# A three-layer block on one Trainium2 core: the opening loads and turns by k tile

## The reference, cut to what matters

```
y  = rms_norm(x, ffn1_pre_g)                 # 256 x 1024
f1 = (silu(y @ w_gate) * (y @ w_up)) @ w_down    # w_gate, w_up: 1024 x 2816
x  = x + 0.5 * rms_norm(f1, ffn1_post_g)
```

## Time and profile before

| | us |
|---|---|
| median of 3 runs | 992.6 (992.57 to 992.99) |
| the profiled execution's own time | 992.94 |
| its span in the trace | 991.1 |
| TensorE busy in the span | 985.8 |
| first real product starts | 7.23 |
| `features` of piece 2 starts | 20.41 |

### The profile page before, as it was taken

How to read it: one execution, slowest core, us unless ns; L and a number is a source line. 1 busy time by engine, 2 the same in 40 slices (tenths; PEclk the granted TensorE clock), 3 DMA queues, 4 the chain that set the end, 5 groups by cost and what they waited for, 6 DMA issues and landing times.

```text
span 991.1 us, 14543 instructions
## 1 busy us (share of the span) xinstructions
PE 985.8 (99%) x5302; PEld 835.6 (84%) x5302; DVE 711.4 (72%) x849; ACT 486.5 (49%) x621; POOL 213.2 (22%) x215
## 2 busy tenths in 40 slices
PE   8999999999999999999999999999999999999998
PEld 6888888888888888888888888888888888888887
DVE  5766767775788767676777998677876767666664
ACT  6534343664665533434545444465555445334342
POOL 3313232014100222222112600060000012223230
PEclk9999999999999999999999999999999999999999
DMA  9665656745325555565745625544536356555561
GB/s 311 227 211 171 208 173 199 268 128 192 127 87 170 203 179 204 176 203 178 240 156 177 204 95 196 190 145 148 170 118 222 129 187 233 170 179 201 179 206 44
DMA packets 121065, 178.53 MB, mean 180 GB/s; under 512 B 5808, under 2 KB 82160, under 8 KB 120896
## 3 DMA queue, kind: packets, MB, share of 16 engines
q1 hardware_dynamic: 120048, 174.86, 52.8%
q0 software_dynamic: 576, 1.39, 0.5%
q10 hardware_dynamic: 400, 1.73, 0.5%
HBM read 176.88 MB, written 2.64 MB: 181 GB/s over the span
## 4 chain that ended last, share of the span: by engine, by line
PE 99%; DMA 0%; ACT 0%; SPq 0%; DVE 0%; issue 0%
PE acc L662 11%; PE acc L666 10%; PE acc L665 10%; PE tp L861 10%; PE gu L861 10%; PE gu L866 5%; PE tp L866 5%; PE tp L662 4%; PE tp L666 4%; PE tp L665 4%; PE gu L662 3%; PE gu L666 3%; PE gu L665 3%; PE acc L1141 2%; PE acc L1144 1%; PE acc L1170 1%
## 5 line engine op out<-in xcount | busy, mean ns | idle before, releaser
L2001 DVE TENSOR_TENSOR wlo<-raw,whi 128x2048 fp32r<-128x2048 f32 x140 | 325.5, 2330 | 153.8 <-ACT whi L1361 152.2
L1361 ACT ACTIVATE whi<-raw 128x2048 fp32r<-128x2048 f32 x150 | 285.8, 1908 | 70.2 <-PE acc L666 22.9
L861 PE MATMUL tp<-act_in,whi 128*128 128x512 f32 x432 | 102.9, 390 | 0.0
L861 PE MATMUL gu<-act_in,whi 128*128 128x512 f32 x432 | 102.6, 390 | 0.0
L1898 POOL TENSOR_TENSOR tmp<-tmp 128x256 f32<-128x256 f32 x54 | 39.8, 737 | 276.2 <-DVE tmp L2122 276.2
L1900 POOL TENSOR_TENSOR sil<-sil,tmp 128x256 f32<-128x256 f32 x54 | 88.7, 1642 | 33.7 <-ACT sil L1432 33.7
L861 PEld LDWEIGHTS gu<-act_in,whi 128*128 128x128 f32 x432 | 80.9, 188 | 16.6
L662 PE MATMUL acc<-whi,hT_hi 128*128 128x512 f32 x240 | 94.0, 392 | 0.0
L665 PE MATMUL acc<-wlo,hT_hi 128*128 128x512 f32 x240 | 93.7, 390 | 0.0
L666 PE MATMUL acc<-whi,hT_lo 128*128 128x512 f32 x240 | 93.4, 389 | 0.0
L861 PEld LDWEIGHTS tp<-act_in,whi 128*128 128x128 f32 x432 | 79.8, 188 | 15.7
(11 more groups left out here) (379 smaller groups left out, 1845.0 us busy)
## 6 DMA issues: line engine op xcount, KB each, us to landing
raw<-in_w_in SPq DMA_DIRECT2D x96, 512.0 KB, 4.5
raw<-in_down SPq DMA_DIRECT2D x66, 512.0 KB, 4.1
raw<-in_gate SPq DMA_DIRECT2D x64, 512.0 KB, 4.3
raw<-in_up SPq DMA_DIRECT2D x64, 512.0 KB, 4.7
raw<-in_w_out SPq DMA_DIRECT2D x16, 512.0 KB, 4.7
raw<-in_w_branch_hg SPq DMA_DIRECT2D x8, 512.0 KB, 4.3
raw<-in_w_branch_attn SPq DMA_DIRECT2D x8, 512.0 KB, 4.7
post<-in_post_gains SPq DMA_DIRECT2D x3, 512.0 KB, 6.0
```

The costliest lines, as they stand in the source:

```text
L861: pe.matmul(banks[:, a, :], w_hi[:, i, a * P:(a + 1) * P], both, start=i == 0, stop=False)
L1361: act.activation(split_weights(k)[0], raw[:, k % RING, :], ACT.Copy).then_inc(hi_ready, 1)
L2001: dve.tensor_tensor(w_lo, raw[:, k % RING, :], w_hi.bitcast(F32), ALU.subtract).then_inc(lo_ready, 1)
```

## The change

SP's list is new. It opens with `fixed`, then gate and up of k tile 0 (128 KB each), gate and up of k tile 1, the second quarter of x's columns for both row halves, then k tiles 2 and 3, then as before. ACT's queue opens with the first quarter of x's columns for t = 0 and t = 1 (128 KB each) and one merged array of one-hot and bias table. SP's list up to the first wait grows from 15 DMAs to 20, for the same bytes. TensorE turns two tiles of t = 0 and two of t = 1 at first, multiplies k tile 0 for both row halves, turns the other four tiles, and goes on by k tile. The bias product moves from ahead of the products to behind the fourth. Piece 1 is rounded in quarters instead of halves. `x_sums` for t = 0 moves behind the last `fills`. The first tiles' PSUM banks are others, and every tile has a semaphore step of its own.

The diff, cut to its core:

```diff
             def first_pieces():
-                x_part(0, 0)
-                half_piece(0, 0)
-                x_part(1, 0)
-                half_piece(0, 1)
+                sp.dma_start(fixed[:, 0:G_END + P], fixed_d[:, 0:G_END + P]).then_inc(head_in, 16)
+                for a in range(2):
+                    first_gate(a)
+                    first_up(a)
+                x_quarter(0, 1)
+                x_quarter(1, 1)
+                for a in (2, 3):
+                    first_gate(a)
+                    first_up(a)
                 x_part(0, 1)
...
                 pe.wait_ge(head_in, 16)
-                turn(0)
-                warm_up(3)
-                pe.wait_ge(bias_parts_in, 16 * 2)
-                pe.matmul(gu[0:8, 1, 0:S], rel[:, :], hot[:, :], start=True, stop=True).then_inc(row_product, 1)
...
+                for i in range(2):
+                    pe.wait_ge(x_first[i], 16)
+                    turn_tile(i, 0)
+                    turn_tile(i, 1)
+                    warm_up(2 - i)
+                pe.wait_ge(tile_lo, 1)
+                pe.wait_ge(part_hi, 1)
+                product(0, 0, 0, rests=(part_lo, 1))
+                pe.wait_ge(tile_lo, 2)
+                product(0, 1, 0)
+                pe.wait_ge(x_in[0], 16)
+                turn_tile(0, 2)
+                pe.wait_ge(x_in[2], 16)
+                pe.wait_ge(tile_lo, 3)
+                turn_tile(1, 2)
+                turn_tile(0, 3)
+                turn_tile(1, 3)
+                pe.wait_ge(part_hi, 2)
+                product(0, 0, 1, rests=(part_lo, 2))
+                pe.wait_ge(tile_lo, 4)
+                product(0, 1, 1)
+                pe.wait_ge(bias_parts_in, 16)
+                pe.matmul(acc[0:8, 1, 0, 0:S], rel, hot, start=True, stop=True).then_inc(row_product, 1)
...
-            first_turned(0, 0, 1, 2)
+            first_turned(0, 0)
             first_hi(0, 0, 1)
-            first_turned(0, 3)
+            first_turned(1, 0)
+            first_turned(0, 1)
             first_hi(0, 1, 1)
+            first_turned(1, 1)
+            first_hi(0, 2, 1)
+            for a in (2, 3):
+                first_turned(0, a)
+                first_turned(1, a)
+            first_hi(0, 3, 1)
             row_from_bank()
-            first_turned(1, 0, 1, 2, 3)
-            first_hi(0, 2, 1)
-            first_hi(0, 3, 1)
-            first_hi(1, 0, 2)
+            first_hi(1, 0, 1)
+            first_hi(1, 1, 1)
             fills(T_FFN1, 2)
+            first_hi(1, 2, 1)
+            first_hi(1, 3, 1)
+            fills(T_FFN1, 3)
             x_sums(0, 0)
-            first_hi(1, 2, 2)
-            fills(T_FFN1, 3)
             hi(2)
...
             fill_scaled(T_FFN1, 2)
-            first_lo(1, 0, 2)
+            first_lo(1, 0, 1)
             fill_rest(T_FFN1, 2)
             fill_scaled(T_FFN1, 3)
-            first_lo(1, 2, 2)
+            for a in range(1, 4):
+                first_lo(1, a, 1)
             fill_rest(T_FFN1, 3)
```

More of the change, by code:

```diff
@@ L172, in build @@
         same = rest[:, C_SAME - P:C_SAME - P + HALF]
-        hot = sb("hot", [REL_BUCKETS, S])
+        bias_parts = sb("bias_parts", [REL_BUCKETS, S + 8])
+        hot, rel = bias_parts[:, 0:S], bias_parts[:, S:S + 8]
         mask16 = sb("mask16", [P, P], BF16)
@@ L228, in build @@
         x_in = [sem(f"x_in{i}") for i in range(2 * TT)]
-        part_in = [sem(f"part_in{i}") for i in range(4)]
+        x_first = [sem(f"x_first{t}") for t in range(TT)]
+        part_in = [sem(f"part_in{i}") for i in range(6)]
         tile_turned, tile_hi, tile_lo = sem("tile_turned"), sem("tile_hi"), sem("tile_lo")
@@ L408, in first_bank @@
         def first_bank(i, a):
-            return tp[:, a // 2, a % 2 * P:(a % 2 + 1) * P] if i else acc[:, a // 2, a % 2, 0:P]
+            banks = (tp[:, 0, :], acc[:, 1, 0, :], acc[:, 0, 1, :], tp[:, 1, :]) if i else \
+                (acc[:, 0, 0, :], acc[:, 0, 1, :], acc[:, 1, 1, :], acc[:, 0, 0, :])
+            return banks[a][:, 0:P]
         def first_place(i, a):
@@ L746, in turn, with turn_tile @@
                     pe.wait_ge(x_in[2 * t + h], 16)
-                    if i >= 2:
-                        fill(u, i, from_x)
-                        return
-                    for a in range(4):
-                        mm = pe.transpose(first_bank(i, a), from_x(t, 4 * h + a), idn)
-                        if a < 3 and (i == 0 or a == 1):
-                            mm.then_inc(tile_turned, 1)
-                    mm.then_inc(turn_full, 1)
+                    fill(u, i, from_x)
+                def turn_tile(i, a):
+                    mm = pe.transpose(first_bank(i, a), from_x(FILLS[u][i][0], a), idn)
+                    mm.then_inc(turn_full if a == 3 else tile_turned, 1)
                 def product(j, t, a, rests=None):
@@ L767, in first_block @@
                 pe.wait_ge(head_in, 16)
[L768 to L783 removed]
+                for i in range(2):
[21 more added lines that the diff above has]
+                pe.matmul(acc[0:8, 1, 0, 0:S], rel, hot, start=True, stop=True).then_inc(row_product, 1)
+                pe.wait_ge(tile_lo, 5)
                 pe.wait_ge(part_hi, 3)
                 product(0, 0, 2, rests=(part_lo, 3))
+                turn(2)
+                pe.wait_ge(tile_lo, 6)
+                product(0, 1, 2)
+                filled(u, 1)
                 pe.wait_ge(hi_ready, 1)
@@ L788, in first_block @@
                 filled(u, 2)
-                product(0, 1, 2)
+                pe.wait_ge(row_copied, 1)
                 turn(3)
@@ L792, in first_block @@
                 filled(u, 3)
-                pe.wait_ge(part_hi, 4)
-                product(1, 0, 0, rests=(part_lo, 4))
-                product(1, 0, 1)
+                for a in range(3):
+                    pe.wait_ge(part_hi, 4 + a)
+                    product(1, 0, a, rests=(part_lo, 4 + a))
                 pe.wait_ge(hi_ready, 2)
-                product(1, 0, 2, rests=(lo_ready, 2))
-                product(1, 0, 3).then_inc(gu_first, 1)
+                product(1, 0, 3, rests=(lo_ready, 2)).then_inc(gu_first, 1)
                 filled(u, 4)
@@ L2440, in first_lo, with first_rest @@
                    .then_inc(lo_ready if a + n == 4 else part_lo, 1)
-            def first_rest(i, *tiles):
-                for a in tiles:
-                    if a == 3 or i and a == 2:
-                        dve.wait_ge(act_hi_ready, i + 1)
-                    else:
-                        dve.wait_ge(tile_hi, 4 if i else a + 1)
-                    hi, rest = first_place(i, a)
-                    ins = dve.scalar_tensor_tensor(out=rest, in0=first_bank(i, a), scalar=first_gain(i, a),
-                                                   in1=hi.bitcast(F32), op0=ALU.mult, op1=ALU.subtract)
-                    ins.then_inc(act_lo_ready if a == 3 else tile_lo, 1)
+            def first_rest(i, a, nth):
+                dve.wait_ge(act_hi_ready if a == 3 else tile_hi, nth)
+                hi, rest = first_place(i, a)
+                dve.scalar_tensor_tensor(out=rest, in0=first_bank(i, a), scalar=first_gain(i, a),
+                                         in1=hi.bitcast(F32), op0=ALU.mult, op1=ALU.subtract)\
+                   .then_inc(act_lo_ready if a == 3 else tile_lo, 1)
             def first_setup():
@@ L2856 @@
           [d[f"down{f}"] for f in range(3)], d["w_in"], d["w_out"], d["w_in_2"], d["w_branch_hg_2"],
-          d["w_branch_attn_2"], d["w_out_2"], d["fixed"], d["packed_rows"], d["post_gains"], d["rel_table"],
-          d["level_masks"], d["one_hot"], out, row, skew)
+          d["w_branch_attn_2"], d["w_out_2"], d["fixed"], d["packed_rows"], d["post_gains"], d["bias_parts"],
+          d["level_masks"], out, row, skew)
     r = run_bass_kernel_spmd(nc, [{"in_" + n: a for n, a in arrays.items()}], core_ids=[0])
```

72 lines of the change are left out of this document (34 added, 38 removed).

## The result

Over 22 runs of each, on the same chip, the changed kernel took 993.91 us in the median (993.62 to 994.47) and the kernel before 992.69 (992.28 to 993.22). The ratio is 1.0013, with a 95% interval of 1.0007 to 1.0018: 1.2 us slower, where 992.4 was forecast, and above the top of the range, 993.3. The difference is inside what I had called "no change", but it is there, and it has the other sign. The profiled execution took 994.33, its span is 992.4, and the granted clock is 1.00.

A forecast was written before the change was run, and what follows sets the result against it. TensorE, fed without a break after 10 us, was taken as the bound. First product 0.58 earlier, stretch 0.4 longer: 0.2 gained, 992.94 to 992.7; median 0.34 below profiled, so 992.4, range 991.7 to 993.3.

The forecast's parts named there:

- Later loads: SP's list: five more DMAs at about 0.5 us each delay later issues; costed at 0, up to 0.5 if backlog empties.
- What is late next: Piece 2's rounding to piece 3's rest: ready 26.15, wanted 26.3; holds by 0.15, caps gains above 0.35 to 0.6.
- the sign of being wrong that the prediction named last: At piece 3 of the weights: the prediction is wrong if TensorE waits for piece 3; no size given.
- s, the first product: TensorE's first product starts at 6.65, 0.58 earlier, 0.80 after up of k tile 0 lands at 5.85.
- Rival 1: First loads: bytes decide, up of k tile 0 lands by 5.5, gain capped at 0.6 to 0.8, time 991.9; chance 0.15.
- The stretch from the first product to `features` of piece 2: TensorE's opening: 13.57 us, 0.4 longer than before, so `features` of piece 2 starts at 20.2, 0.2 earlier.
- The bias product: TensorE's opening: now among products instead of filling a wait, it costs a step of about 0.5.
- Order of products: First products: 0.26 wait inside the first as before, 0.2 more for the second's tile rest and slower restart.
- end of the opening: Last four products before `features` of piece 2: TensorE waits 0.25 for DVE's `fill_rest`, where before there was no wait.
- Rival 3, the clock: Opening: TensorE's clock falls while idle, products step at 0.43 not 0.23; +1.2 to +2.6, time 993.8 to 995.2; chance 0.07.
- The sum: Whole kernel: 992.94 profiled less 0.2 is 992.7; median 0.34 below the profiled one, so 992.4, no tellable change.

The follow-up runs named there:

- moved bias product: Changed kernel with x's second quarters issued on ACT's queue, plus the bias product in place of the last junk matmul; median 993.17, ratio 1.0003.
- late tiny DMAs: Kernel before with five 1 KB DMAs added to SP's list behind the twelfth issue, directly ahead of piece 2's DMAs; median 992.87, ratio 1.0001.
- kernel with the quarters on ACT's queue: Changed kernel with the two DMAs of x's second quarters issued on ACT's queue instead of SP's; median 993.15, ratio 1.0005.
- early tiny DMAs: Kernel before with five 1 KB DMAs added to SP's list behind the third issue; median 993.87, ratio 1.0012.

## Why the prediction was wrong, point by point

*Later loads: the step that failed.* The prediction put five more DMAs into SP's list and costed them at 0, because "these transfers queue for bytes, not for their issue"; it had the rate of issue (262 GB/s) beside the rate of the engines (342) and gave "up to 0.5 us" if the backlog ran dry. It ran dry, and not for a moment: 283 and 297 GB/s from 3.4 to 13 us, where issues of 128 KB give 279. Piece 2's rounding came 1.97 us late. The reading error is plain in hindsight. The 8 us between issue and landing of piece 2 and the share of 1.04 are properties of a queue that is fed 256 KB per issue; they say nothing on what is left of the backlog once the pieces are halved. The comparison had to be made at the start of the queue, where no backlog exists yet. That this is a cause is shown twice. Two issues taken out of SP's list brought the windows back to 339 and 350 GB/s, piece 2's rounding to 16.29 and the median down by 0.8. And the same 2.3 us of issuing cost 1.2 us early and 0.2 late. It is not the whole miss: with the two issues gone the median, 993.15, is still 0.8 above the forecast.

*What is late next: right in mechanism, decisive in effect.* The prediction gave the chain piece 2's rounding + 5.34 + 4.23 + 0.15 for piece 3, and 0.15 of room. With 17.97 it gives 27.69, and 27.59 was measured; with 16.53 of the second profile of the moved bias product 26.25 (26.15), with 17.22 of the late tiny DMAs 26.94 (26.84). In the kernel before the chain ended at 25.57 and TensorE came at 26.52; with 0.05 from the one to the other, as measured here, the room was 0.9. So 1.97 late at piece 2 less 0.9 is the 1.07 lost at `features` of piece 3. This is also the sign of being wrong that the prediction named last: TensorE waited for piece 3, 0.33 us. The prediction had the chain as a cap on gains, and did not run it the other way, as the path by which a late piece 2 reaches the total. What the prediction missed beside it is the landing of piece 3, which stood only 0.2 ahead of the chain before, and 0.5 in the changed kernel.

*s, the first product.* Forecast 6.65 (6.3 to 7.0), measured 6.12: below the bound, and below the 6.2 that the prediction had named as a sign of being wrong. Up of k tile 0, issued at 1.67, had landed by 5.3, 3.7 after its issue, where I took 5.85. Rival 1 (bytes decide) had the time right, 5.5 or before, but in part by luck. All the bounds were read from one profile in which the first transfers landed late. In the late tiny DMAs' kernel, whose list is the old one up to 7.11, up of k tile 0 with its 256 KB landed at 5.8 and the first product started at 6.60. Against that the changed kernel is 0.48 earlier, close to the 0.58 that the sum forecast; the rest of the miss is the profile that it started from.

*The stretch from the first product to `features` of piece 2.* Forecast 13.57, measured 21.15 - 6.12 = 15.03. The bias product took 0.52 as forecast (0.5). The excess lies in PE's timeline: 0.46 in the first product (three steps of 0.61, 0.31 and 0.23), of which the forecast had 0.26, for another reason; 0.16 ahead of the turns at 11.37; 0.38 ahead of those at 13.63, with a wait for x; 0.48 ahead of 15.27, with a wait for the rest of a tile that ACT handed on late, behind the weights it waited for. In the kernel with the quarters on ACT's queue the last three are gone, and the same stretch was 19.85 - 6.17 = 13.68. So they go back to the late loads.

*Order of products, end of the opening.* 13.68 against 13.57 is how well the sum did once the loads flow, with some luck in the terms: the wait ahead of the last four products, put at 0.25, shows there as steps of 0.29 and 0.33 where 0.23 is the rule, 0.16 in all, and slower restarts behind turns and the bias product make up the difference. In the changed kernel itself the terms could not be seen.

*Rival 3, the clock.* Its price did not fall on the changed kernel, whose only trace of it is the first product's step of 0.61. But the mechanism is real and stood close: behind 1.7 us of idle TensorE, one load order away, the products ran at 1.2 GHz for 3 us.

*The sum.* The medians differ by 1.22. 1.07 of this is seen at `features` of piece 3. The profiled runs differ by 1.39: besides, 0.23 in the remaining span and 0.09 outside of it. The 0.23 isn't the change's, as far as can be told: the late and early tiny DMAs, whose program after the opening is that of the kernel before, have 0.28 and 0.30 there (991.7 - 26.84 and 992.0 - 27.12 against 964.58). The part outside the span (0.1 here, 0.3 in the new order with the old loads) stays open. So does what is left once the loads flow: the two profiles with the quarters on ACT's queue start `features` of piece 3 0.56 and 0.39 ahead of the profiled run of before, but end only 0.33 and 0.12 ahead of it, and their kernel's median is 0.46 above the kernel before. That is the cost of the new order which no experiment here takes apart.

## What to carry to other kernels

Where transfers are cut finer to get the first one sooner, divide the bytes of one DMA by the issue interval of its queue, and compare that with the rate at which the DMA engines move; if it is less, expect the later transfers to fall behind, as here by 2 us, and a backlog seen in the old profile is no cover, because the cut is what keeps it from building up. The same issue time cost 1.2 us here where the queue was empty and 0.2 behind a backlog. And run the chain of "what is late next" in both directions: the room that caps a gain is also all that stands between a late load and the total. Last, take bounds on landings from more than one profile: here those of one and the same list lay up to 0.8 us apart.

## What the runs showed of the hardware

- In the first 4.5 us an issue on SP's or ACT's queue took 0.38 to 0.47 us whatever the size: 1 KB (five in 2.31 us) and 256 KB alike. Later ones could take longer: up to 0.86 for 256 KB, up to 1.48 for 512 KB, and 0.51 to 1.62 for the 240 KB block. At one in 0.47 us, 128 KB each give 279 GB/s, and 283 was measured. The Trainium skill ("DMA: Bandwidth & Descriptors", the section on issuing engines not being separate DMA queues) says that issuing from several engines only saves the sequencer's issue time, and calls that usually small beside the DMA itself. The runs agree with the first. The second doesn't hold here: 0.47 us of issue stand beside 131,072 B / 346 GB/s = 0.38 us of moving, and in this opening that was the thing to save: two issues moved to ACT's queue brought 283 GB/s to 339 and 322 in two profiles, and 0.8 us.
- The moment at which TensorE's clock rises at the start moves from kernel to kernel. The junk matmuls step by 0.43 to 0.45 until 5.4 in the changed kernel, and its first product begins with a step of 0.61; with the quarters on ACT's queue that step is 0.31 in both profiles, and in the kernel before the steps are 0.22 from 5.62 on the earlier trace rows. The granted clock reads 1.00 in all of these.
- The granted clock did not show the low level that the clock starts with: it read 1.00 over the first seven junk matmuls of every kernel, and also with the old order and the new loads, whose products still stepped by 0.42 to 0.43 up to 13.6. It showed the one fall from the high level, with the new order and the old loads: 0.50 from 8 to 10.6 us. The steps tell the level in both cases.
- Runs of the kernels with quarters on ACT's queue spread by 1.0 to 1.5 us, those of the kernel before by 0.8 to 1.3 and those of the changed kernel by 0.85.
- With the list of before, the landing of the first transfers moved from run to run: 109 KB took 4.3, 3.6 and 3.5 us from issue to landing, and 256 KB of x 4.1, 3.4 and 3.3, in the profiles of the kernel before and of the two with 1 KB DMAs.
